# Tiles on 128-byte steps, slot transposes behind the scatter, and gathered rows split a turn earlier

## The reference

```
for l in 0, 1:
    h = rms_norm(x);  project h @ w_in[l] into three attentions and gates
    x = x + W_out( sum_i sigmoid(gate_i) * (y_i @ W_branch_i) )
    h = rms_norm(x)
    x = x + swiglu(h)                                        (l = 0, width 3584)
    x = x + sum over the two chosen experts e of w_e * swiglu_e(h)      (l = 1)
out = rms_norm(x)
```

## Time and profile before

| | |
|---|---|
| median of 3 runs | 1810.45 us (1808.38 to 1810.64) |
| profiled execution: its time | 1810.18 us |
| its span (first to last instruction) | 1808.4 us |
| PE busy | 1754.6 us, 97% |
| DVE busy | 1389.7 us, 77% |
| ACT busy | 1189.8 us, 66% |
| data moved | 479 MB, mean 265 GB/s |

### The profile page before, as it was taken

How to read it: one execution, slowest core, us unless ns; L and a number is a source line. 1 busy time by engine, 2 the same in 40 slices (tenths; PEclk the granted TensorE clock), 3 DMA queues, 4 the chain that set the end, 5 groups by cost and what they waited for, 6 DMA issues and landing times.

```text
span 1808.4 us, 28962 instructions
## 1 busy us (share of the span) xinstructions
PE 1754.6 (97%) x9812; PEld 1511.7 (84%) x9812; DVE 1389.7 (77%) x1506; ACT 1189.8 (66%) x1419; POOL 23.6 (1%) x49
## 2 busy tenths in 40 slices
PE   7999999999999999989999999999999999999997
PEld 6888899999988888878888888888888888788886
DVE  6675475455466755689989899899899899898996
ACT  5465544444445655467777777777777778777775
POOL 2000000000000000000000000000000000000000
PEclk9999999999999999989999999999999999999999
DMA  8544366666655434869989999999999899899990
GB/s 324 161 117 117 120 231 189 186 186 185 185 179 161 114 108 136 291 222 369 374 308 373 346 334 371 335 347 371 325 358 372 312 369 371 308 374 343 334 372 24
DMA packets 213867, 479.20 MB, mean 265 GB/s; under 512 B 14768, under 2 KB 16832, under 8 KB 213296
## 3 DMA queue, kind: packets, MB, share of 16 engines
q1 hardware_dynamic: 212592, 474.80, 75.9%
q0 software_dynamic: 1216, 3.61, 0.7%
HBM read 475.20 MB, written 3.15 MB: 265 GB/s over the span
## 4 chain that ended last, share of the span: by engine, by line
PE 89%; ACT 4%; issue 3%; DVE 3%; DMA 0%; POOLq 0%; POOL 0%; ACTq 0%; DVEq 0%
PE ps L1651 81%; PE ps L2021 2%; PE ps L2054 1%; PE ps L1878 1%; ACT probs L1003 1%; PE ps L1861 1%; PE ps L1848 1%; ACT whi L868 1%; PE ps L1703 1%; PE ps L1850 0%; DVE wlo L1176 0%; ACT probs L995 0%; DMA gain<-in_g_mem 0%; DVE act_m L1599 0%; ACT gates L1036 0%
## 5 line engine op out<-in xcount | busy, mean ns | idle before, releaser
L1176 DVE TENSOR_TENSOR wlo<-raw,whi 128x1024 fp32r<-128x1024 f32 x766 | 915.1, 1219 | 304.6 <-ACT whi L868 274.4
L868 ACT ACTIVATE whi<-raw 128x1024 fp32r<-128x1024 f32 x766 | 797.2, 1055 | 328.0 <-PE ps L1651 317.9
L1651 PE MATMUL ps<-whi,xg_hi 128*128 128x512 f32 x896 | 358.2, 400 | 2.4 <-DVE xg_lo L1182 2.4
L1651 PE MATMUL ps<-wlo,xg_hi 128*128 128x512 f32 x896 | 352.1, 393 | 0.0
L1651 PE MATMUL ps<-whi,xg_lo 128*128 128x512 f32 x896 | 349.8, 390 | 0.0
L1651 PE MATMUL ps<-hT_hi,whi 128*128 128x256 f32 x896 | 258.1, 288 | 4.2 <-ACT gates L878 2.9
L1651 PE MATMUL ps<-hT_lo,whi 128*128 128x256 f32 x896 | 252.9, 282 | 0.0
L1651 PE MATMUL ps<-hT_hi,wlo 128*128 128x256 f32 x896 | 252.3, 282 | 0.0
L1651 PEld LDWEIGHTS ps<-wlo,xg_hi 128*128 128x128 f32 x896 | 168.9, 188 | 38.6
L1651 PEld LDWEIGHTS ps<-whi,xg_hi 128*128 128x128 f32 x896 | 169.2, 189 | 38.0 <-DVE wlo L1176 5.4
L1651 PEld LDWEIGHTS ps<-whi,xg_lo 128*128 128x128 f32 x896 | 169.1, 189 | 35.3
(11 more groups left out here) (313 smaller groups left out, 2200.7 us busy)
## 6 DMA issues: line engine op xcount, KB each, us to landing
raw<-in_w_down_exp SPq DMA_DIRECT2D x200, 512.0 KB, 5.1
raw<-in_w_gate_exp SPq DMA_DIRECT2D x184, 512.0 KB, 4.9
raw<-in_w_up_exp SPq DMA_DIRECT2D x160, 512.0 KB, 5.3
raw<-in_w_in SPq DMA_DIRECT2D x72, 512.0 KB, 3.7
kM<-in_w_up_exp SPq DMA_DIRECT2D x40, 512.0 KB, 5.6
raw<-in_w_gate_dense SPq DMA_DIRECT2D x28, 512.0 KB, 4.4
raw<-in_w_up_dense SPq DMA_DIRECT2D x28, 512.0 KB, 4.3
raw<-in_w_down_dense SPq DMA_DIRECT2D x28, 512.0 KB, 4.2
```

Of the source, the lines that this page charges most:

```text
L868: s.activation(whi[n % SPLIT][:, 0:w], raw[tile(key)][:, 0:w], ACT.Copy).then_inc(chunk_hi, 1)
L1176: v.tensor_tensor(wlo[n % SPLIT][:, 0:w], raw[tile(key)][:, 0:w], whi[n % SPLIT][:, 0:w].bitcast(F32), ALU.subtract).then_inc(chunk_split, 1)
L1651: ins = mm(o, lhsT, rhs, start=start and i == 0, stop=stop and i == 2, skip_group_check=True)
```

## The change

Three edits, which do not depend on each other's results:

1. Tiles with at least 128 numbers in a partition start at a multiple of 128 bytes, smaller ones at a multiple of 16.
2. T_back moves from behind G/U group 1 to directly behind the scatter, before the transposes of group 0. It reads `onehot_next`, which still holds the current expert, and writes the second bank of `ps[1]`. `onehot`, `cur` and one of the two calls of `slots_of` go. DVE copies `slot_w` and `back` after `add_scattered`, and `moe_rest(0)` now comes ahead of `add_scattered`.
3. The split of the gathered rows moves from the head of the turn to the end of the turn that gathered them, behind the splits of D group 6; for the first expert it stands before the loop, ahead of the first two chunks.

```
             def tensor(name, shape, dt=F32):
+                line = 128 if math.prod(shape[1:]) >= 128 else 16
+                return scope.enter_context(nc.sbuf_tensor(name, shape, dt, align_bytes=line))
...
 ACT:
+            def gathered_hi(turn):
+                for half in range(2):
+                    eng.wait_ge(psum_full[3], gathered_by(turn, half))
+                    s.activation(xg_hi[:, 4 * half:4 * (half + 1), :].rearrange("p k n -> p (k n)"),
+                                 ps[3][:, 512 * half:512 * (half + 1)], ACT.Copy).then_inc(hi_copied, 1)
+            gathered_hi(0)
             with s.Fori(0, turns) as e:
-                upto(2)
-                for half in range(2):
-                    eng.wait_ge(psum_full[3], gathered_by(e, half))
-                    s.activation(xg_hi[...], ps[3][...], ACT.Copy).then_inc(hi_copied, 1)
                 upto(4)
...
                 upto(FFN_CHUNKS)
+                gathered_hi(e + 1)
...
 DVE:
+            gathered_lo(0)
             with v.Fori(0, turns) as e:
-                upto(2)
-                for half in range(2):
-                    rest(("gather", half), xg_lo[...], ps[3][...], xg_hi[...], e)
                 upto(4)
...
                 upto(before_split(0))
+                moe_rest(0)
                 add_scattered(e)
-                moe_rest(0)
-                upto(before_split(0) + 2)
-                slots_of(e, cur, e * 2 + 1, onehot)
+                eng.wait_ge(back_full, e + 1)
+                v.tensor_copy(slot_w[:, :], ps[1][:, FF_GROUP + TOK:FF_GROUP + TOK + 1])
+                v.tensor_copy(back[:, :], ps[1][:, FF_GROUP:FF_GROUP + TOK])
                 upto(before_split(0) + 4)
-                slots_of(e + 1, cur_next, e * 2 + 2, onehot_next)
+                slots_of(e + 1)
                 for g in range(1, GROUPS):
                     upto(before_silu(g))
                     moe_product(g)
-                    if g == 1:
-                        wait_full(eng, ("T_back",), e)
-                        v.tensor_copy(slot_w[:, :], ps[1][:, TOK:TOK + 1])
-                        v.tensor_copy(back[:, :], ps[1][:, 0:TOK]).then_inc(psum_free[1], 1)
...
                 upto(FFN_CHUNKS)
+                gathered_lo(e + 1)
...
 PE, behind G/U group 0:
                             scatter(e)
+                            slots = onehot_next[:, :, :].bitcast(F32)
+                            for t in range(NT):
+                                mm(ps[1][:, FF_GROUP + TOK:FF_GROUP + TOK + 1], slots[:, t, :], cur_next[:, 2 + t:3 + t],
+                                   start=t == 0, stop=t == NT - 1)
+                            for t in range(NT):
+                                ins = nc.tensor.transpose(ps[1][:, FF_GROUP + P * t:FF_GROUP + P * (t + 1)], slots[:, t, :],
+                                                          ident[:, :])
+                            ins.then_inc(back_full, 1)
                             transposed_act(0)
-                        if g == 1:
-                            pe.wait_ge(routed_sem, tl.after("routed", "onehot", e))
-                            wait_free_in_loop(pe, ("T_back",), e)
-                            ... the same four instructions with onehot, cur and ps[1][:, 0:TOK + 1]
```

More of the change, by code:

```diff
@@ L1 @@
+import math
 from contextlib import ExitStack
@@ L269, in build_tally @@
                 tl.add("psum_full3", ("gathered", "first", half))
+            for half in range(2):
+                areas["gather", half] = 3
+                tl.add("hi_copied", ("gathered", "first", half))
+                tl.add("psum_free3", ("gathered", "first", half))
             experts_from[0] = tl.count["chunk"]
             tl.enter_loop()
-            for half in range(2):
[L274 to L277, removed]
             tl.add("routed", "onehot_next")
@@ L289, in build_tally @@
                         split(("moe", "T", 0), 1)
-                    if g == 1:
-                        psum(("T_back",), 1)
                 elif g + 1 < GROUPS:
@@ L295, in build_tally @@
                 tl.add("psum_full3", ("gathered", "next", half))
+                tl.add("hi_copied", ("gathered", "next", half))
+                tl.add("psum_free3", ("gathered", "next", half))
             tl.leave_loop(EXPERTS)
@@ L366, in sb_in, with tensor @@
         def sb_in(scope):
-            return lambda name, shape, dt=F32: scope.enter_context(nc.sbuf_tensor(name, shape, dt))
+            def tensor(name, shape, dt=F32):
+                line = 128 if math.prod(shape[1:]) >= 128 else 16
+                return scope.enter_context(nc.sbuf_tensor(name, shape, dt, align_bytes=line))
+            return tensor
         sb = sb_in(ctx)
@@ L511, in trunk_kernel @@
         route = sb("route", [P, 2 * EXPERTS + 1, 4])
-        cur = sb("cur", [P, 4])
         cur_next = sb("cur_next", [P, 4])
@@ L517, in trunk_kernel @@
         turns_i = sb("turns_i", [P, 1], I32)
-        onehot = sb("onehot", [P, NT, SLOTS])
         onehot_next = sb("onehot_next", [P, NT, SLOTS], F32R)
@@ L588, in trunk_kernel @@
         routed_sem = sem("routed")
+        back_full = sem("back_full")
         stored = sem("stored")
@@ L617, in wait_read, with gathered_by @@
             eng.wait_ge(counters[name], tl.after(name, event, it))
-        def gathered_by(turn, half):
-            per_turn = tl.events["psum_full3", ("gathered", "next", half)][1]
-            return turn * per_turn + tl.after("psum_full3", ("gathered", "first", half))
+        def gathered_by(turn, half, name="psum_full3"):
+            per_turn = tl.events[name, ("gathered", "next", half)][1]
+            return turn * per_turn + tl.after(name, ("gathered", "first", half))
         def area(key):
@@ L1127, in moe_hi @@
                                  ACT.Copy).then_inc(hi_copied, 1)
-                upto(2)
-                for half in range(2):
-                    eng.wait_ge(psum_full[3], gathered_by(e, half))
-                    s.activation(xg_hi[:, 4 * half:4 * (half + 1), :].rearrange("p k n -> p (k n)"),
-                                 ps[3][:, 512 * half:512 * (half + 1)], ACT.Copy).then_inc(hi_copied, 1)
                 upto(4)
@@ L1564, in _, with slots_of, gathered_lo @@
             turns = v.value_load(turns_i[0:1, 0:1], min_val=EXPERTS, max_val=2 * EXPERTS)
-            def slots_of(e, tile_, name, dst):
-                v.tensor_copy(tile_[:, :], route[:, bass.ds(e, 1), :].rearrange("p a b -> p (a b)")).then_inc(picked, 1)
-                eng.wait_ge(picked, name)
+            def slots_of(e):
+                v.tensor_copy(cur_next[:, :], route[:, bass.ds(e, 1), :].rearrange("p a b -> p (a b)")).then_inc(picked, 1)
+                eng.wait_ge(picked, e)
                 for t in range(NT):
-                    ins = v.tensor_scalar(dst[:, t, :], iotaS[:, :], tile_[:, t:t + 1], None, ALU.is_equal)
+                    ins = v.tensor_scalar(onehot_next[:, t, :], iotaS[:, :], cur_next[:, t:t + 1], None, ALU.is_equal)
                 ins.then_inc(routed_sem, 1)
+            def gathered_lo(turn):
+                for half in range(2):
+                    part = slice(4 * half, 4 * (half + 1))
+                    eng.wait_ge(hi_copied, gathered_by(turn, half, "hi_copied"))
+                    v.tensor_tensor(xg_lo[:, part, :].rearrange("p k n -> p (k n)"), ps[3][:, 512 * half:512 * (half + 1)],
+                                    xg_hi[:, part, :].rearrange("p k n -> p (k n)").bitcast(F32),
+                                    ALU.subtract).then_inc(psum_free[3], 1)
             def y_rest(cols):
@@ L2045, in _ @@
             with nc.tensor.Fori(0, turns) as e:
-                pe.wait_ge(psum_free[3], tl.after("psum_free3", ("gather", 0), e))
+                pe.wait_ge(psum_free[3], gathered_by(e, 0, "psum_free3"))
                 def transposed_act(g):
@@ L2064, in _ @@
                                 if which == "G" and g == 0 and c == 2:
-                                    pe.wait_ge(psum_free[3], tl.after("psum_free3", ("gather", 1), e))
+                                    pe.wait_ge(psum_free[3], gathered_by(e, 1, "psum_free3"))
                                 ins = moving_chunk(("moe", which, g, c), lambda kk, t: xg_hi[:, 2 * c + kk, :],
@@ L2070, in _ @@
                             scatter(e)
-                            transposed_act(0)
-                        if g == 1:
-                            pe.wait_ge(routed_sem, tl.after("routed", "onehot", e))
-                            wait_free_in_loop(pe, ("T_back",), e)
[L2076 to L2080, removed]
+                            slots = onehot_next[:, :, :].bitcast(F32)
[6 more added lines that the diff above has]
+                            ins.then_inc(back_full, 1)
+                            transposed_act(0)
                     else:
```

## The result

| | before | changed |
|---|---|---|
| median of 6 runs each, side by side | 1808.95 us (1807.78 to 1810.64) | 1816.68 us (1814.49 to 1817.09) |
| ratio, 95% interval | | 1.0039 [1.0026, 1.0052] |
| span of the profiled execution | 1808.4 us | 1814.9 us |
| seven turns, start of the transposes of group 0 to the next | 126.02 to 126.05 us | 126.42 to 126.84 us, mean 126.64 |

The changed kernel is slower, by 7.7 us, where 20 us of gain were forecast.

A forecast was written before the change was run, and what follows sets the result against it. PE was taken to bound the kernel, busy 125.08 of a turn's 126.05 us. The terms -3.5 - 5.0 + 0 + 4.0 - 4.2 - 7 - 4 = -19.7 us took 1810.18 to 1790.5 us, range 1768 to 1808.

The forecast's parts named there:

- The loop's placement: Expert loop, 4,032 matmuls with stationary tiles moved from 64 to 0: 1 ns less each, -4 us.
- The rival that ended at 1815: Expert loop: stationary start 0 is as bad as 96, costing 21 us; total about 1815 us, chance 0.08.
- The dense 512-column matmuls: Dense parts, 816 matmuls with stationary tiles moved from 96 to 0: 5.2 ns less each, -4.2 us, bound 0.
- The 256-column matmuls: 3,504 matmuls, mostly with hT, moving tiles from 96 to 0: 2 ns less each, -7 us, bounds 0 and -22.8.
- The turn's head: Start of turns 2 to 8: PE no longer waits for the gathered rows' split, 0.5 us each, -3.5 us.
- T_back: Between scatter and transposes it hides in PE's idle time, 0.63 us in each of 8 turns: -5.0 us.
- DVE's order: DVE copies slot_w and back before chunk 12, leaving 0.17 us: cost 0, upper bound 2.4 us.
- The first turn: Gather to first product: PE starts 4.6 us later, partly at half clock; +4.0 us, bounds 2.5 and 7.7.
- the near case of 3.4: First turn: the clock rises 3.4 us behind PE's new start, a loss of 4.0 us.
- The far case: First turn: the clock rises 11.6 us behind PE's new start, a loss of 7.7 us.
- the rival of 1811.8: Late clock rise costs 7.7 us, late chunk 12 costs 2.4, placement gains nothing: no change, chance 0.04.
- Placement does nothing: All tiles: the 5.2 ns have another cause, only -4.5 us of schedule remain; 1805.7 us, chance 0.2.

The follow-up runs named there:

- align_only: The kernel before with only the new tile alignment, engine order as before: 1821.74 us, ratio 1.0065.
- sched_only: The changed kernel with the old 32-byte tile placement, so only the two order changes remain: 1805.86 us against 1809.75, ratio 0.9977.
- all_128: The changed kernel with all six xg and actm tiles at 128 modulo 512 bytes: 1794.41 us against 1809.73 for the kernel before, ratio 0.9918.
- tback_only: The kernel before with only T_back moved behind the scatter, and DVE's order with it: 1806.59 us against 1810.09, ratio 0.9983.
- shift_w: The changed kernel with whi and wlo at 0 modulo 256, xg at 128, even actm at 0, odd at 64: 1815.55 us, one run.
- head_one: The changed kernel with xg and actm at 128 modulo 512, gathered rows split at the turn's head behind one chunk: 1791.89 us, ratio 0.9903 to the kernel before.

## Why the prediction was wrong

**The loop's placement: the step that failed.** "4,032 matmuls of the experts, stationary from 64 to 0 ... The tile nearer to a boundary was the faster one; I take 1 ns: -4 us". It had the sign wrong. Measured +3.8 ns (align_only), 8 turns x 1.93 = +15.4 us; in the changed kernel, against sched_only, a turn is 126.64 - 124.97 = 1.67 us longer, +13.4 over 8. The observation under it, 229.1 against 234.3 ns, was sound; the reason read into it, distance of the stationary tile from its own boundary, was not. `whi` and `wlo` were left out of the comparison because they don't move. They are its other half: 96 bytes behind them is slow, 64 ahead is nearly good, 128 away is slow, 0 is best. The rival that ended at 1815 named "stationary tiles that start where `whi` starts" as the bad place, by modulo 128. Its time came true by luck: of its terms, +21 for the loop was +13.4, -7 for the 256-column matmuls was 0, and the two misses nearly cancelled; its reason is the opposite of what the runs show. Between the forecast of -19.7 and the +6.5 of the spans lie 26 us: 17.4 of them are this step, 7 the 256-column matmuls, 1.2 the dense ones.

**The dense 512-column matmuls**: -4.2 predicted, "at least as good as 64". The distance went from 234.2 ns to between 226.8 and 228.1, by the tile, 5.7 us for all 816. At the first gather 3.0 us of it are seen in the changed kernel and 4.1 in all_128. PE runs the same instructions up to there, so the starts can be compared one by one, before against changed:

- PE's first matmul starts at 9.57 against 9.86: 0.3 us lost.
- A stretch of half clock of 3.4 us at 42.7, which the trace of before has not: 43.06 in both, then 44.77 against 46.14, 1.4 us lost.
- Another at 305.5: 305.81 against 305.85, then 307.60 against 308.98, 1.3 us lost.
- The one at 762.6 is gone, but gives back only 0.5 us (759.20 against 756.69, then the router at 767.10 against 764.11), as PE waits there for DVE in both.

-5.7 + 0.3 + 1.4 + 1.3 - 0.5 = -3.2, and 3.0 are measured. The two new stretches as windows of the changed kernel (columns as in the earlier trace rows):

```profile
42.70:46.10 3.40, 3.04 (x7) 2.48 (x8) 3.40 (x6) 2.79 (x6) 0.00 (x0) 0.50 0.00 0
305.50:308.90 3.40, 3.05 (x14) 3.05 (x15) 3.40 (x4) 1.20 (x2) 0.00 (x0) 0.50 0.51 146
```

The stretch at 42.7 occurs in tback_only too, with the old placement. The one near 305 is in the traces of all nine kernels with edit 1's alignment and in none of the three others; why was not looked into.

**The 256-column matmuls**: -7 predicted, 0 measured, the lower bound. Distances that had scattered from 116 to 125 ns became an even 120: equal starts (0 instead of 96) took the scatter out and left the mean, 119.9 ns over the intervals up to 130 ns. Equal starts are not the best here: in shift_w, with 128 bytes between them, the mean is 119.0 for `hT` and 118.6 for `y`, some 3 us over the 3,504. Of the 6.5 ns between 120.0 and the router's 113.5, about 1 could be had by placement in these runs.

**The turn's head**: -3.5 predicted; 7 x 0.507 = -3.5 (sched_only). **T_back**: -5.0 predicted, bounds 4.3 and 5.0; 8 x 0.59 = -4.7 by the usual turn, -4.5 summed (tback_only). **DVE's order**: 0 predicted with 0.17 us left to chunk 12; 0.28 left and no wait. **The first turn**: +4.0 predicted; +4.0 and +4.1. The chain was the predicted one, table load included; the start moved by 4.5 us (from the gather's start 11.37 us instead of 6.85, predicted 4.6), and the clock rose 3.6 us behind the new start, which is the near case of 3.4. (The far case was summed too low: with the rise at 789.7 + 11.6 = 801.3, PE would do 5.7 us less than at full clock from 789.9 on, which with the 2.5 makes 8.2, not 7.7. Only the rival of 1811.8 used it, which so comes to 1812.3.) So the schedule's part was right in each step: -4.5 forecast, -3.9 measured and -4.4 by the spans.

**Rivals.** "Placement does nothing" is out: the distances follow a tile's start in every run, on unchanged code. "The first turn eats the schedule" is nearly true of edit 3 alone (-3.5 + 4.0), not of both. The Trainium skill (SBUF — State Buffer, "Specifications (TRN2)") has lines of 16 bytes; the tiles of these matmuls started on multiples of 32 in both kernels, and it still mattered where. By the figure of its page TensorE: Matmul & The Clock Gate ("Wait — 56ns, not 53.3ns?"), columns over 2.4 GHz plus about 2.5 ns, 512 columns take 215.8 ns as an estimate; no loop here reached that, and the best is 226.7. The same page ("Step-by-step: what each phase is for") says that PE reads weights and streamed data through two ports of their own, so that loading one doesn't slow the other. The runs don't bear this out for these tiles: the interval depends on how the starts of the two lie to each other, though no run shows where they meet.

**What stays open.** Why the difference matters, why 64 and 16 bytes ahead are better than 32 ahead or anything behind, and why a difference can have two levels. That two reads collide on something repeating every 256 bytes fits the table; it was only argued.

## What to carry over

When an alignment is changed, write down where stationary *and* moving tile start modulo 256 bytes and look at the pair: equal starts were best for the 512-column matmuls, not for the 256-column ones, and "a rounder number" for one of them cost 15 us. Judge matmuls by the distance from start to start, not by their duration, and judge a split moved out of a loop's head by its first turn too, where nothing hides it. An explanation found by comparing two tiles should be asked what third thing both are compared with.

## What the runs showed of the hardware

- 512-column fp32r matmuls, each with its own weight load of 128 columns: 226.7 to 228.9 ns with equal starts modulo 256 bytes, 232 to 234 with most others. A duration on the page says little of it: 395 ns for `whi,xg_lo` at 233, 389 for `mixT` at 227.
- The level goes by the group. In a stretch of 24 or 48 matmuls it is constant, then another one may hold, by the same tiles. In sched_only, with the old placement, one group with its D group ran at 233.3 ns in four of the turns and the next again at 229; 72 x 4.4 = 0.32 us is the whole difference between its turns of 124.79 and 125.11 us. The same placement so cost 1.93 us a turn in align_only and 1.67 in the changed kernel, where more groups stood at 232.3 and fewer at 233.4. The two levels in sched_only:

```profile
930.14 0.40 PE L1659 MATMUL ps<-whi,xg_lo 128*128 128x512 f32 x1
...
940.88 0.40 PE L1659 MATMUL ps<-wlo,xg_hi 128*128 128x512 f32 x1
...
947.38 0.39 PE L1659 MATMUL ps<-whi,xg_lo 128*128 128x512 f32 x1
...
957.90 0.39 PE L1659 MATMUL ps<-wlo,xg_hi 128*128 128x512 f32 x1
```

- In all eight kernels that split the gathered rows ahead of the loop, PE paused for 4.3 us at half clock, and the stretch of half clock took 20.5 us. Where the first product followed the gather at once it took 17.0 to 17.1 (before, align_only, head_one), and 13.6 in tback_only, where it began later, at 776.7.
